# Rounded weight panels in rows of 260 columns instead of 256, four slots 4,160 bytes apart

## The reference, cut to what matters

```python
xn = _rmsnorm(h, norm1_g[l])
proj = xn @ w_in[l]
...
ya = _from_heads_padded(oa) @ w_a_o[l]
...
mix = (jax.nn.sigmoid(g_a + gbias[:D_MODEL]) * ya
       + jax.nn.sigmoid(g_b + gbias[D_MODEL:2 * D_MODEL]) * yb
       + jax.nn.sigmoid(g_c + gbias[2 * D_MODEL:]) * yc)
h = h + mix @ w_o[l]
u = _causal_dwconv(_rmsnorm(h, norm2_g[l]) @ w_up[l], mlp_conv_w[l])
u_gate, u_up = jnp.split(u, 2, axis=-1)
h = h + (jax.nn.silu(u_gate) * u_up) @ w_down[l]
return _rmsnorm(h, final_norm_g)[:, N_META:]
```

## Time and profile before

| | |
|---|---|
| median of 3 runs | 1746.51 us |
| lowest, highest | 1746.36 us, 1746.97 us |
| span of the profiled execution | 1745.1 us |
| TensorE busy with matmuls | 1734.3 us, 99% |
| VectorE busy | 1117.8 us, 64% |
| ScalarE busy | 763.7 us, 44% |
| mean DMA rate | 184 GB/s |
| granted TensorE clock, 1005 to 1490 us and 1510 to 1730 us | 1.00, its upper level of 2.4 GHz |

### The profile page before, as it was taken

One profiled execution on the slowest core, in us unless ns is written; L12 is line 12 of the kernel. 1 busy time (PEld: TensorE's weight loads), 2 busy tenths in 40 slices (PEclk: granted clock), 3 DMA queues, 4 the chain that ended last, 5 costly groups with the idle time before them and its releaser, 6 DMA issues.

```text
span 1745.1 us, 34098 instructions
## 1 busy us (share of the span) xinstructions
PE 1734.3 (99%) x13429; PEld 1680.7 (96%) x13429; DVE 1117.8 (64%) x1607; ACT 763.7 (44%) x921; POOL 263.3 (15%) x494
## 2 busy tenths in 40 slices
PE   9999999999999999999999999999999999999998
PEld 8999999999999999999999999999999999888886
DVE  6857766667565554555556687777777777554454
ACT  6635444354354444444444444334444444343433
POOL 3153332630530000000000043321000000000000
PEclk9999999999999999999999999999999999999999
DMA  8567557666565655556645566666555565665654
GB/s 232 169 180 186 168 149 198 176 175 178 153 184 181 189 178 178 175 182 194 201 159 192 181 195 192 204 200 192 183 182 181 180 186 180 223 190 189 189 192 134
DMA packets 310296, 320.62 MB, mean 184 GB/s; under 512 B 17353, under 2 KB 285133, under 8 KB 310093
## 3 DMA queue, kind: packets, MB, share of 16 engines
q1 hardware_dynamic: 296861, 311.01, 58.2%
q0 software_dynamic: 12928, 7.80, 2.0%
q10 hardware_dynamic: 432, 0.79, 0.1%
HBM read 311.10 MB, written 2.11 MB: 179 GB/s over the span
## 4 chain that ended last, share of the span: by engine, by line
PE 99%; DVE 0%; DMA 0%; ACT 0%; SPq 0%; issue 0%; ACTq 0%; DVEq 0%
PE ps L1435 27%; PE ps L1437 27%; PE ps L1436 27%; PE ps L1693 5%; PE ps L1692 5%; PE ps L1691 5%; PE ps L1526 0%; DMA xb<-in_x_dram 0%; PE ps L1540 0%; PE ps L1565 0%; PE ps L1555 0%; PE ps L1556 0%; PE ps L1584 0%; PE ps L1585 0%; DVE xl L941 0%; DVE lo L896 0%
## 5 line engine op out<-in xcount | busy, mean ns | idle before, releaser
L896 DVE TENSOR_TENSOR lo<-raw,hi 128x1024 fp32r<-128x1024 f32 x584 | 709.9, 1229 | 494.4 <-ACT hi L627 490.2
L1435 PE MATMUL ps<-xh,hi 128*128 128x260 f32 (+1 forms) x3328 | 945.8, 284 | 0.2 <-DVE xl L941 0.2
L1437 PE MATMUL ps<-xh,lo 128*128 128x260 f32 (+1 forms) x3328 | 941.7, 283 | 0.0
L1436 PE MATMUL ps<-xl,hi 128*128 128x260 f32 (+1 forms) x3328 | 936.5, 281 | 0.0
L627 ACT CAST hi<-raw 128x1024 fp32r<-128x1024 f32 x584 | 604.8, 1048 | 671.8 <-PE ps L1437 539.0
L1436 PEld LDWEIGHTS ps<-xl,hi 128*128 128x128 f32 x3328 | 626.6, 188 | 0.2
L1435 PEld LDWEIGHTS ps<-xh,hi 128*128 128x128 f32 x3328 | 625.2, 188 | 1.3 <-issue 0.4
L1437 PEld LDWEIGHTS ps<-xh,lo 128*128 128x128 f32 x3328 | 624.7, 188 | 0.0
L610 POOL DMA_DIRECT2D hT<-h2b x128 | 69.6, 553 | 604.3 <-DVE h2b L1289 599.7
L1693 PE MATMUL ps<-lo,act_h 128*128 128x512 f32 x350 | 138.5, 396 | 0.0
L1692 PE MATMUL ps<-hi,act_l 128*128 128x512 f32 x350 | 137.3, 392 | 0.0
(11 more groups left out here) (298 smaller groups left out, 1383.6 us busy)
## 6 DMA issues: line engine op xcount, KB each, us to landing
raw<-in_w_in_dram SPq DMA_DIRECT2D x224, 512.0 KB, 3.6
raw<-in_w_up_dram SPq DMA_DIRECT2D x176, 512.0 KB, 4.6
raw<-in_w_down_dram SPq DMA_DIRECT2D x88, 512.0 KB, 4.7
raw<-in_w_o_dram SPq DMA_DIRECT2D x32, 512.0 KB, 3.4
raw<-in_w_in_dram SPq DMA_DIRECT2D x32, 256.0 KB, 4.2
raw<-in_w_a_o_dram SPq DMA_DIRECT2D x16, 512.0 KB, 4.3
raw<-in_w_b_o_dram SPq DMA_DIRECT2D x16, 512.0 KB, 3.3
raw<-in_w_c_o_dram SPq DMA_DIRECT2D x16, 512.0 KB, 3.3
```

Of the source, the lines that this page charges most:

```text
L896: nc.vector.tensor_tensor(part(ph, i, q, lo_all), raw[:, s, :], part(ph, i, q, hi_all).bitcast(F32), ALU.subtract).then_inc(lo_ready, 1)
L1435: nc.tensor.matmul(acc, w_hi, mh, start=first and j == 0, stop=False)
L1436: nc.tensor.matmul(acc, w_hi, ml, start=False, stop=False)
L1437: ins = nc.tensor.matmul(acc, w_lo, mh, start=False, stop=last and j == KJ - 1)
```

## The change

`WROW` = 260 columns now lie from one row `j` of a rounded panel to the next, of which 256 are filled and 4 (16 bytes) are left empty. A slot is `WSLOT` = 4 x 260 = 1,040 columns, 4,160 bytes. `DPAD` goes from 128 to 64 columns, so that `hi` and `lo` keep their sizes (64 + 4 x 1,040 = 128 + 4 x 1,024 = 4,224 columns), and every other tensor keeps its address. `raw` and the loads into it are unchanged. ScalarE and VectorE now write four runs of 256 columns instead of one of 1,024. In the down-projection the panels stay contiguous and keep the shift of 16 bytes, in slots that are 4,160 bytes apart. Only its first three panels, which stand in slots as `UP` lays them out, are read as two runs of 256 columns with the gap between them. The fourth is contiguous and unshifted. No instruction is added, removed or put in another place on any engine: TensorE's list is the same row by row, and on ScalarE and VectorE only the shape written by L627 and L896 differs, 128x4x256 for 128x1024, outside the down-projection.

```diff
-DAT, DPAD = 4, 128
+DAT, DPAD = 4, 64
+WROW = COLS + 4
+WSLOT = KJ * WROW
...
-        hi_all = sb("hi", [P, DPAD + SLOTS * KJ * COLS], F32R)
+        hi_all = sb("hi", [P, DPAD + SLOTS * WSLOT], F32R)
...
-            at = DPAD + ph.slot(q) * KJ * COLS - (DAT if ph is DN and i * DN.n + q >= SLOTS else 0)
-            return buf[:, at:at + KJ * COLS]
+            s = ph.slot(q)
+            if ph is DN:
+                at = DPAD + s * WSLOT - (DAT if i * DN.n + q >= SLOTS else 0)
+                return buf[:, at:at + KJ * COLS].rearrange("p (j n) -> p j n", n=COLS)
+            return buf[:, DPAD + s * WSLOT:DPAD + (s + 1) * WSLOT].rearrange("p (j n) -> p j n", j=KJ)[:, :, 0:COLS]
...
         def streamed(i, q, buf):
-            return part(DN, i, q, buf).rearrange("p (j n) -> p j n", n=DCOLS)
+            if i == 0 and q < LOOK:
+                return part(UP, 0, q, buf).rearrange("p (j h) n -> p j h n", h=2)
+            at = DPAD + DN.slot(q) * WSLOT - (DAT if i * DN.n + q >= SLOTS else 0)
+            return buf[:, at:at + KJ * COLS].rearrange("p (j h n) -> p j h n", h=2, n=COLS)
...
         def tiles(buf, s, j, n):
-            return buf[:, s, j * COLS + n * P:j * COLS + (n + 1) * P]
+            return buf[:, s, j * WROW + n * P:j * WROW + (n + 1) * P]
...
-                nc.scalar.copy(part(ph, i, q, hi_all), raw[:, s, :]).then_inc(hi_ready, 1)
+                nc.scalar.copy(part(ph, i, q, hi_all), panel(raw, s)).then_inc(hi_ready, 1)
...
-                nc.vector.tensor_tensor(part(ph, i, q, lo_all), raw[:, s, :], part(ph, i, q, hi_all).bitcast(F32),
+                nc.vector.tensor_tensor(part(ph, i, q, lo_all), panel(raw, s), part(ph, i, q, hi_all).bitcast(F32),
                                         ALU.subtract).then_inc(lo_ready, 1)
...
-                    acc, tok = ps[:, 2 * st + b, :], slice(b * P, (b + 1) * P)
+                    acc, tok = ps[:, 2 * st + b, :].rearrange("p (h n) -> p h n", h=2), slice(b * P, (b + 1) * P)
```

More of the change, by code:

```diff
@@ L173, in hybrid_layer @@
         raw = sb("raw", [P, SLOTS, KJ * COLS])
-        hi_all = sb("hi", [P, DPAD + SLOTS * KJ * COLS], F32R)
+        hi_all = sb("hi", [P, DPAD + SLOTS * WSLOT], F32R)
         hi = hi_all[:, DPAD:].rearrange("p (s n) -> p s n", s=SLOTS)
-        lo_all = sb("lo", [P, DPAD + SLOTS * KJ * COLS], F32R)
+        lo_all = sb("lo", [P, DPAD + SLOTS * WSLOT], F32R)
         lo = lo_all[:, DPAD:].rearrange("p (s n) -> p s n", s=SLOTS)
@@ L1687, in down_rows @@
                     kt = (q % DQ) * DK + j
-                    w_hi, w_lo = streamed(i, q, hi_all)[:, j, :], streamed(i, q, lo_all)[:, j, :]
-                    acc, tok = ps[:, 2 * st + b, :], slice(b * P, (b + 1) * P)
+                    w_hi, w_lo = streamed(i, q, hi_all)[:, j], streamed(i, q, lo_all)[:, j]
+                    acc, tok = ps[:, 2 * st + b, :].rearrange("p (h n) -> p h n", h=2), slice(b * P, (b + 1) * P)
                     end = kt == FT - 1 or (last and q == DN.n - 2 and j == DK - 1)
@@ L1696, in last_columns @@
             def last_columns(half):
-                cols, tok = slice(half * HC, (half + 1) * HC), slice(P, 2 * P)
+                tok = slice(P, 2 * P)
                 acc = AUX[half][:, 0:HC]
@@ L1700, in last_columns @@
                     kt = FT - DK + j
-                    w_hi, w_lo = (streamed(DN.trips - 1, DN.n - 1, buf)[:, j, cols] for buf in (hi_all, lo_all))
+                    w_hi, w_lo = (streamed(DN.trips - 1, DN.n - 1, buf)[:, j, half] for buf in (hi_all, lo_all))
                     nc.tensor.matmul(acc, act_h[:, kt, tok], w_hi, start=j == 0, stop=False)
```

## The result

The changed kernel takes 1758.7 us (median of 3 runs, 1758.54 to 1760.43) against 1746.5 us before. The ratio is 1.0072, with a 95% interval of 1.0056 to 1.0088: it is slower by 12 us. The forecast was 1746.5 us with a range of 1734 to 1756 us, so the time lies outside it.

What follows compares the result with a forecast made beforehand. It took TensorE's matmul pace as the bound. Zero each for weight tiles, down-projection and rounding left the profiled 1745.1 us; the median lies 1.4 us above, giving 1746.5 us, range 1734 to 1756 us.

Steps and rivals of the forecast that it cites:

- The bound: Whole kernel: TensorE's distance from one matmul start to the next sets the time; loads, rounding and splitting are hidden.
- Rounding, splitting and the gap: ScalarE's and VectorE's four-run writes stay hidden, taken as zero; the gap in three down-projection panels costs at most 0.2 us.
- Weight tiles at other places: 11,904 matmuls with stationary panels, 1,424 us: moving their weight tiles was taken as nothing, with 10.7 us either way for range.
- the slope: From 260 to 512 columns: 0.445 ns per added column, so the loss was put on the stream, leaving 3.2 ns a load.
- the 10.6 and 17.7 ns: Loss per matmul over one column a cycle: 260 columns in the up-projection, 512 in the down-projection.
- The down-projection: Its panels move only by whole 64-byte steps, by the slot: 1.8 us up or down, taken as zero.
- The slower one: Rival: stream-to-tile distance matters, odd multiples of 16 bytes are good; two weight rows lose 1%, 1752.0 us, chance 0.20.
- The faster one: Rival: weight tiles at four places keep stream and tile out of step, gaining 10.7 us, 1735.8 us; chance 0.34.

Runs made afterwards that it cites:

- load64: Kernel before with stationary tiles of 64 columns instead of 128 for most matmuls of the up- and down-projection; 1748.9 us against 1746.9.
- s32: Kernel before with all rounded panels in hi and lo 32 bytes lower; 1752.4 us (ratio 1.0031).
- x32: Kernel before with a 32-byte gap ahead of the activations, so xh, xl, bo, mix and act move up and the weight panels stay; 1753.0 us (ratio 1.0034).
- slots_only: Changed kernel with rows put back to 256 columns while slots stay 4,160 bytes apart; 1750.8 us (ratio 1.0023).
- rows32: Changed kernel with 264 columns to a row and slots 4,224 bytes apart; 1762.6 us (ratio 1.0091).
- s16: Kernel before with all rounded panels in hi and lo 16 bytes lower; 1750.6 us (ratio 1.0023).
- s48: Kernel before with all rounded panels in hi and lo 48 bytes lower; 1755.7 us (ratio 1.0050).
- slots128: Changed kernel with rows of 256 columns and slots 4,224 bytes apart; 1753.2 us (ratio 1.0037).
- s64: Kernel before with all rounded panels in hi and lo 64 bytes lower; 1746.95 us (ratio 1.0004).
- dat8: Kernel before with DAT = 8: only the down-projection's panels from the fifth on move, by 16 bytes more; 1744.7 us (ratio 0.9987).

## Why the prediction was wrong

**The bound: right.** It was TensorE's pace alone, before and after. The number and the order of the matmuls are the same, and no wait was added.

**Rounding, splitting and the gap: right.** Both helpers take what they took (1,047 and 1,229 ns), and the first three panels of the down-projection show no price of their gap (232.2 ns against 233.3).

**Weight tiles at other places: this is the step that failed.** The prediction took from the slope that the loss over one column a cycle belongs to the stream, and went on from there to "nothing" for the place of the weight tiles. Of the first half, this much held: with half the load the pace stays (load64), so the 10.6 and 17.7 ns aren't paid for the load's columns. That they belong to the stream by itself isn't shown. The second half doesn't follow from it, and is false. s32 moved the tiles and x32 the streams, both have the same distances between the two, and they agree in all three stretches. No place tried removes the loss, but the place moves the pace by some 1% for 260 columns and 2% for 512. I had the row that says so the earlier trace rows, 1.0% for 16 bytes, and could have seen that "its distance to the stationary tiles moved too" was open; I let an argument on the mean decide a question on the spread.

**What the change cost, by its parts.** For the 260 columns it is 119.93 - 118.88 = 1.05 ns. The rows stand at four distances now. When all rows have them, these cost 118.88, 119.70, 119.17 and 119.55 ns, a mean of 119.33: 0.45 ns. The slots standing 64 bytes apart cost 0.36 ns (slots_only). If the two add up, 0.24 ns are left, which go with rows32's finding that rows which stand unlike each other cost more than their mean. Over 10,560 matmuls, 1.05 ns would be 11.1 us. By the starts in the two traces these matmuls lost 10.5 us together and the 272 columns 0.3, while the first panel had started 0.4 us earlier than before. The shares are sums of separate runs and so an estimate. Rows of 260 columns in slots that stand alike weren't tried, so how the loss divides between rows and slots stays open.

**The down-projection: right mechanism, undersized.** I bounded its 64-byte steps at 1.8 us either way and took zero. It lost 1.4 us, as with the slots alone (slots_only), nearly all of it in two of the four slots (232.9 and 234.6 ns).

**The rivals.** The slower one had the right quantity, the distance, and the wrong rule. It took odd multiples of 16 for good and priced only two of four rows, 5.5 us; s16 to s48 show four different values in no such order, and it did not see the cost of slots or of unlikeness. The faster one, four places to keep stream and load out of step, is refuted: all four layouts whose tiles stand unlike each other (the changed kernel, slots_only, slots128, rows32) are slower than the kernel before, by 4 to 16 us.

**The range.** I had bounded the weight tiles' part at 10.7 us, up or down, but used that for the lower end alone. The upper end was to be the slower rival's price doubled. That sum gives 1746.5 + 2 x 5.5 = 1757.5 us and not 1756, and falls short either way. My own bound upwards, with that of the down-projection, would have been 1746.5 + 10.7 + 1.8 = 1759.0 us and holds the result. That 10.7 comes so near to what the tiles' part lost (10.5 + 0.3 us) is in part luck: it stands for three rows that lose 1% each, and the runs show a loss shared by rows, slots and their unlikeness.

**The two read ports.** The Trainium skill, on its page "SBUF — State Buffer", section "Who interferes with whom", has two read ports of TensorE that are independent of each other. Here the distance between what the two read changes the pace by up to 2% (228.9 to 233.3 ns for 512 columns), and in x32 by 1% (231.1 to 233.3 ns) with the stream itself unmoved. Where the page and this differ, the measurement decides.

## What to carry to other kernels

Where TensorE is busy throughout and streams one 32-bit column a cycle, treat the distance in memory between the stationary tiles and the stream as a tuning value. Shift one buffer by multiples of 16 bytes and time each; here the best place was worth 2.2 us, in the down-projection, and the worst multiple of 16 cost 9 us in the whole kernel, a half step of 8 bytes 13 us. Keep all tiles at the same distance: each of the four layouts that skewed rows or slots to "spread" the accesses was slower than the kernel before. And an argument on where a loss comes from doesn't bound what a shift can do to it: one row that shows a shift matter outweighs it.

## What the runs showed of the hardware

- A matmul of 512 columns runs at one of a few paces. Uniform layouts had 228.9, 231.1 and 233.3 ns, steps of 2.2 ns, with two exceptions: s64 had 231.7, and the first four panels of s48 230.0. In dat8, the kernel before and s32 a group of three matmuls takes 686.7, 693.3 and 700.0 ns on the mean by their starts, which is 103, 104 and 105 times 16 cycles at 2.4 GHz. A panel of 24 matmuls of 260 columns takes 428 times 16 cycles in the kernel before (24 x 118.88 ns) and 429 in s32. What is counted in 16 cycles there isn't settled; 16 columns of 4 bytes are 64 bytes.
- The pace is exact: before the change all undisturbed panels of 260 columns took 2.853 us to within 1 or 2 ns, in all phases, whatever ScalarE, VectorE and the DMAs did.
- Loading 64 columns instead of 128 took 139 ns instead of 188 in the rows, with a tenth of full loads in the mean, and changed the pace by under 0.5%.
- The loss over one column a cycle, 228.9 - 213.3 = 15.6 ns at the best place, stays open: no run took it away.
